# Gate tiles moved into five heads' turns, and one shared stationary key tile per score level for both chunks

## The chip, the core and the metric

The kernel runs on one core of a Trainium2 chip. Its engines work side by side and meet through semaphores: TensorE (PE) multiplies, VectorE (DVE), ScalarE (ACT) and GpSimd (POOL) work element by element, and SyncE (SP) issues DMA transfers. The metric is the device time of one execution in microseconds (us); lower is better. A kernel's time is the median of its runs.

## What is computed

One step of a decoder layer over 320 token columns: one prompt of 256 tokens and 8 samples of 8 tokens, width 2048, everything in float32. After a norm, one input projection with 5120 columns feeds a pooling mixer (1024 columns) and eight heads of a gated recurrence, 128 columns each for q, f, v (called i below) and the gate g. Both groups go through an output projection and a residual add, and then come a SwiGLU block with 5632 hidden columns and a last norm.

```python
u, q, f, i, g = split(rms_norm(x, norm1) @ w_in)
forget = lb + (1 - lb) * sigmoid(f)
k, v, q = 1 - forget, i, silu(q)
# per head and token: S_t = diag(forget_t) S_{t-1} + k_t^T v_t ;  o_t = q_t S_t
o, S_new = hgrn2_recurrence(q, k, v, log(forget), S_prev)
o = rms(o) * hg_norm * silu(g)
x = x + concat([pool_mix(u), o]) @ w_o
x = x + (silu(h2 @ w_gate) * (h2 @ w_up)) @ w_down        # h2 = rms_norm(x, norm2)
```

## The kernel before

**Dense tiles.** Activations lie in SBUF with features on partitions and the 320 tokens along the free axis. Every large product is cut into *units* (`unit`): one 128-column weight tile, 16 row blocks, and for each block three fp32r matmuls of 320 columns (high part of the weights with both parts of the activations, low part with the high part), so 48 matmuls. A unit's weight tile is loaded by SP into one of two buffers `w_raw`, ACT writes its high part `w_hi` in two pieces (`split_hi`), and DVE then writes the low part `w_lo` = `w_raw` - `w_hi` in two pieces (`split_lo`, `lo_piece`). Two PSUM banks take turns, and a unit may start only when the unit two before it has been read out; `unit_read` counts these reads.

**Order of the input projection.** Eight pooling units, then three units per head (f, q, v; the numbers H0 on), then eight gate units (G0 on), then sixteen units of the output projection (O0 on), then the SwiGLU block.

**A head.** In `window(n, parity, h, r)` each engine interleaves the three units of head h with the recurrence of the head before it, r. The recurrence is evaluated by levels: for each of 7 levels (block halves of 1, 2, ..., 64 tokens) the keys are scaled towards the end of their block and the queries from its start. The pieces, by the names in the traces:

- DVE reads the unit f out (`zf`), ACT makes the forget factors (`t`), DVE multiplies them up in `products` (seven small operations `t<-t`, semaphore `prod_ready`).
- POOL makes the keys in `keys`: `kx0` = 1 - forget, and for each level the next `kx` by one multiplication with `t`; then `query` (`qq<-zq,sgm`, the silu of q), then `key_copies` (written to `dg`), and, first in the next window, `rec_sample` (`sn<-s,t`, 1024 elements per partition, and `vm`). POOL works in this order.
- DVE scales the queries in `queries`: `qr0` and seven further levels, eight operations, the first of which waits for `qq`.
- PE multiplies in `rec_scores`: transposes of the last keys, then for every level and each of the two 128-token chunks of the prompt one matmul with the chunk's own `kx` level as stationary operand and the 64 queries of the right block halves moving; own-token and sample scores lie between; at the end transposes of v. It waits for `qr_ready` and `kx_ready`.
- DVE puts the scores into place with 12 predicated copies (`rec_scores` on DVE, `sc`, `scs`), and PE goes on with `rec_state`, `rec_out`, `rec_stat` (means of squares). DVE turns these into the norm (`rec_rms`, which ends with the diagonals `dg`), and `rec_bcast` on PE spreads them over the partitions: PE waits for `dg` there. `rec_norm` and `rec_lo` write the head's result.

`rec_scores` stands in the middle of the window's first unit on PE, `rec_state` behind it, `rec_out` in the middle of the second, `rec_stat` behind it, `rec_bcast` behind the third.

**A gate.** In `gate`, DVE reads the unit out, ACT takes its sigmoid, POOL multiplies (`zq<-zf,sgm`), DVE adds up the head's high and low part and multiplies (`gate_apply`), ACT writes the new high part and DVE the new low part. Nothing else runs beside most of the gate units.

What sets the order on each engine is the order of the code; nothing is scheduled.

Of the kernel before, what the change touches and what calls it, by code (L numbers as in the profile page):

```python
# [54 lines left out]
C_MP = C_ID + P  # L55
# [8 lines left out]
G0 = H0 + 3 * HEADS  # L64
O0 = G0 + HEADS
# [6 lines left out]
def constant_table(np):  # L72

    c = np.zeros((P, C_END), np.float32)
    c[:, C_ID:C_ID + P] = np.eye(P)
    s = np.arange(P)[:, None]
    for level in range(LP):
# [3 lines left out]
        for ch in range(NC):  # L81
            c[:, C_MP + level * P + ch * 64:C_MP + level * P + ch * 64 + 64] = m
# [10 lines left out]
def hybrid_kernel(nc, x_prompt, x_sample, cache_pool, state_hgrn, lb_param, norm1, w_in, w_pool, pool_scale,  # L93
# [12 lines left out]
    with ctx:  # L106
# [56 lines left out]
        kx = region(early, [(f"kx{l}", [P, N if l <= LS else TP], F32) for l in range(LP + 1)])  # L163
# [16 lines left out]
        go = vv  # L180
# [34 lines left out]
        zf_sig, f_ready, prod_ready, zq_sig, q_ready, qr_ready, kx_ready = (  # L215
            sem(n) for n in ("zf_sig", "f_ready", "prod_ready", "zq_sig", "q_ready",
                             "qr_ready", "kx_ready"))
# [26 lines left out]
        def thrice(rep, src):  # L244

            return (rep[:, 0:6 * HS].rearrange("p (i c t) -> p i c t", i=2, c=3),
                    src[:, TP:N].rearrange("p (i t) -> p i t", i=2).unsqueeze(2).to_broadcast([P, 2, 3, HS]))
# [13 lines left out]
        def times(level, n, lo):  # L261

            m = n // 2 ** (level + 1)
            return tl[level][:, 0:m, lo:lo + 2].unsqueeze(3).to_broadcast([P, m, 2, 2 ** level])

        def prod_in(level, which):

            m = (N if level < LS else TP) // 2 ** (level + 1)
            return tl[level][:, 0:m, which:which + 1].rearrange("p (m a) q -> p m (a q)", a=2)

# [21 lines left out]
        def _(sp):  # L292
# [21 lines left out]
            sp.dma_start(cst[:, C_MP:C_END], consts[:, C_MP:C_END]).then_inc(masks_loaded, 16)  # L314
# [5 lines left out]
            with sp.Fori(0, HEADS // 2) as i:  # L320
                for k in range(2):
                    for j, part in enumerate((2, 1, 3)):
                        load(H0 + 6 * i + 3 * k + j, (3 * k + j) % 2, win_v, (0, KD),
                             part * PW + (2 * i + k) * P)
            with sp.Fori(0, HEADS // 2) as i:
                for k in range(2):
                    load(G0 + 2 * i + k, k, win_v, (0, KD), 4 * PW + (2 * i + k) * P)
# [22 lines left out]
        def _(pe):  # L350
# [141 lines left out]
            def rec_scores(r):  # L492
# [3 lines left out]
                pe.transpose(TK[:, 0:P], kx[LP][:, 0:P], ident)  # L496
                pe.transpose(TK[:, P:TP], kx[LP][:, P:TP], ident)
# [7 lines left out]
                def level(bk, at, l):  # L505
                    for c in range(NC):
# [65 lines left out]
            def window(n, par_, r, extra=(None, None), last=False):  # L572

                def at(f):
                    return (lambda: f(r)) if r is not None else None
# [1015 lines left out]
```

## Time and profile before

| | us |
|---|---|
| median of 3 runs (1488.51 to 1493.13) | 1489.78 |
| the profiled execution's own time | 1493.66 |
| its span, first to last instruction | 1491.4 |
| PE / DVE / ACT / POOL busy in the span | 1460.7 / 804.9 / 550.8 / 188.2 |

The busy sums are of the whole span. The recurrence takes the stretch from about 122 us (scores of head 0) to 395 us (last spread of head 7); before and behind it PE runs dense units without a break. A matmul's record begins when it is issued and its end is modelled, so on PE the distance from start to start tells what one costs. One fp32 matmul leaves two records, one fp32r matmul one.

### The profile page before, as it was taken

The numbers are of one execution on the slowest core, as the hardware profiler recorded it, in microseconds if no ns is written. First come the engines' busy times: TensorE is split into PE (matmuls) and PEld (weight loads), VectorE is DVE, ScalarE is ACT, GpSimd is POOL, SyncE is SP. The second block draws the span as 40 slices with busy tenths as digits, with TensorE's granted clock in tenths as the row PEclk, the third lists the DMA queues.
The fourth block names the chain that finished last, engine by engine and source line by source line (L and its number), as shares of the span: only waits on it lengthen the run. The fifth ranks groups of instructions, "written<-read, shape, count | busy, mean of one in ns | idle before, by whom it ended". The sixth has DMA issues, their size and how long they took to land.

```text
span 1491.4 us, 27027 instructions
## 1 busy us (share of the span) xinstructions
PE 1460.7 (98%) x9928; PEld 1440.6 (97%) x9928; DVE 804.9 (54%) x1200; ACT 550.8 (37%) x823; POOL 188.2 (13%) x202
## 2 busy tenths in 40 slices
PE   7999999999999999999999999999999999999996
PEld 5999999999999999999999999999999999999996
DVE  4657788787665554444444444444444444444443
ACT  6443433344443343333333333333333333333443
POOL 0244434333112210000000000000000000000131
PEclk9999999999999999999999999999999999999998
DMA  8445444434455555554565555565554556555453
GB/s 222 136 127 143 128 127 131 114 114 138 114 162 143 153 144 153 141 160 125 146 187 142 141 142 141 144 164 153 157 141 134 151 146 164 154 151 141 119 148 114
DMA packets 409519, 214.52 MB, mean 144 GB/s; under 512 B 4093, under 2 KB 407757, under 8 KB 409420
## 3 DMA queue, kind: packets, MB, share of 16 engines
q1 hardware_dynamic: 391207, 203.52, 49.8%
q10 hardware_dynamic: 18277, 10.52, 2.5%
q8 instruction: 23, 0.38, 0.1%
q14 instruction: 12, 0.10, 0.0%
HBM read 206.14 MB, written 7.89 MB: 144 GB/s over the span
## 4 chain that ended last, share of the span: by engine, by line
PE 85%; DVE 9%; issue 3%; ACT 2%; DMA 1%; DVEq 0%; ACTq 0%; SPq 0%
PE bank L366 27%; PE bank L367 27%; PE bank L368 27%; DVE qr L1190 2%; DVE w_lo L1013 2%; DVE t L1177 1%; ACT w_hi L682 1%; DVE sc L1205 1%; PE bank L507 1%; DMA xt<-in_x_sample 1%; DVE sn L1249 0%; PE bank L462 0%; PE bank L410 0%; PE bank L538 0%; PE bank L412 0%
## 5 line engine op out<-in xcount | busy, mean ns | idle before, releaser
L366 PE MATMUL bank<-a_hi,w_hi 128*128 128x320 f32 x2048 | 642.4, 314 | 0.0
L367 PE MATMUL bank<-a_lo,w_hi 128*128 128x320 f32 x2048 | 636.1, 311 | 0.0
L368 PE MATMUL bank<-a_hi,w_lo 128*128 128x320 f32 x2048 | 635.9, 311 | 0.0
L1013 DVE TENSOR_TENSOR w_lo<-w_raw,w_hi 128x1024 fp32r<-128x1024 f32 (+1 forms) x416 | 467.3, 1164 | 150.3 <-ACT w_hi L682 149.5
L682 ACT ACTIVATE w_hi<-w_raw 128x1024 fp32r<-128x1024 f32 (+1 forms) x416 | 387.3, 967 | 158.6 <-PE bank L368 148.5
L366 PEld LDWEIGHTS bank<-a_hi,w_hi 128*128 128x128 f32 x2048 | 387.6, 189 | 2.4
L367 PEld LDWEIGHTS bank<-a_lo,w_hi 128*128 128x128 f32 x2048 | 387.7, 189 | 0.8
L368 PEld LDWEIGHTS bank<-a_hi,w_lo 128*128 128x128 f32 x2048 | 387.3, 189 | 0.0
L366 PE MATMUL bank<-h_hi,w_hi 128*128 128x320 f32 x704 | 217.7, 309 | 0.0
L367 PE MATMUL bank<-h_lo,w_hi 128*128 128x320 f32 x704 | 216.6, 308 | 0.0
L368 PE MATMUL bank<-h_hi,w_lo 128*128 128x320 f32 x704 | 216.5, 308 | 0.0
L367 PEld LDWEIGHTS bank<-h_lo,w_hi 128*128 128x128 f32 x704 | 132.0, 187 | 0.0
L366 PEld LDWEIGHTS bank<-h_hi,w_hi 128*128 128x128 f32 x704 | 132.0, 187 | 0.0
L368 PEld LDWEIGHTS bank<-h_hi,w_lo 128*128 128x128 f32 x704 | 131.9, 187 | 0.0
L1562 POOL TENSOR_TENSOR sq<-x 128x320 f32<-128x320 f32 x15 | 10.8, 720 | 903.1 <-DVE x L1399 903.1
L909 ACT ACTIVATE h_hi<-hid 128x320 f32 (+1 forms) x44 | 20.7, 472 | 238.3 <-DVE hid L1367 238.3
L1401 DVE TENSOR_TENSOR x_res<-x_res,bank 128x320 f32 (+1 forms) x48 | 23.4, 488 | 120.7 <-PE bank L368 120.7
L1022 DVE TENSOR_TENSOR zu<-bank,rms_bc 128x320 f32<-128x320 f32 x44 | 21.6, 491 | 120.3 <-PE bank L368 120.3
L905 ACT ACTIVATE sg<-zg 128x320 f32<-128x320 f32 x44 | 20.8, 472 | 175.5 <-DVE zg L1022 175.5
L1022 DVE TENSOR_TENSOR zg<-bank,rms_bc 128x320 f32<-128x320 f32 x44 | 21.6, 491 | 86.4 <-PE bank L368 86.3
L1498 POOL TENSOR_TENSOR kx<-kx,t 128x256 f32<-128x256 f32 (+1 forms) x56 | 48.7, 870 | 30.8 <-DVE t L1177 27.5
L366 PE MATMUL bank<-mp_hi,w_hi 128*128 128x320 f32 x128 | 39.4, 308 | 0.0
(218 smaller groups left out, 1186.5 us busy)
## 6 DMA issues: line engine op xcount, KB each, us to landing
w_raw<-in_w_gate SPq DMA_DIRECT2D x44, 1024.0 KB, 5.6
w_raw<-in_w_up SPq DMA_DIRECT2D x44, 1024.0 KB, 5.6
w_raw<-in_w_down SPq DMA_DIRECT2D x64, 704.0 KB, 4.8
w_raw<-in_w_in SPq DMA_DIRECT2D x39, 1024.0 KB, 5.8
w_raw<-in_w_o SPq DMA_DIRECT2D x16, 1024.0 KB, 6.1
s<-in_state_hgrn ACTq DMA_DIRECT2D x8, 512.0 KB, 4.3
out<-sn ACTq DMA_DIRECT2D x8, 512.0 KB, 7.2
xt<-in_x_prompt SPq DMA_DIRECT2D x3, 512.0 KB, 9.4
```

The lines of the kernel that those rows point to most:

```text
L366: pe.matmul(out, whi[:, par_, cols], r_hi, start=(k == 0), stop=False)
L367: pe.matmul(out, whi[:, par_, cols], r_lo, start=False, stop=False)
L368: last = pe.matmul(out, wlo[:, par_, cols], r_hi, start=False, stop=(k == last_k))
L507: last = pe.matmul(bk[:, at + c * 64:at + c * 64 + 64].rearrange("p (m j) -> p m j", j=2 ** l), kx[l][:, c * CH:(c + 1) * CH], right_half( ...
L682: act.activation(whi[:, par_, k0 * P:k1 * P], raw[:, par_, k0 * P:k1 * P], ACT.Copy)\
L905: act.activation(sg[:, :], zg[:, :], ACT.Silu).then_inc(gate_act, 1)
L909: act.activation(h_hi[:, j, :], hid[:, :], ACT.Copy).then_inc(hid_hi, 1)
L1013: dve.tensor_tensor(wlo[:, par_, cols], raw[:, par_, cols], whi[:, par_, cols].bitcast(F32), SUB)\
L1022: return dve.tensor_tensor(out, zb[par_][:, 0:N], rbc[:, :], MUL)
L1190: dve.tensor_tensor(blocks_of(qr[l + 1], l, n), blocks_of(qr[l], l, n), times(l, n, 0), MUL)\
L1401: dve.tensor_tensor(x1[:, j, :], x1[:, j, :], zb[par_][:, 0:N], ADD).then_inc(unit_read, 1)
L1498: pool.tensor_tensor(blocks_of(kx[l + 1], l, n), blocks_of(kx[l], l, n), times(l, n, 2), MUL)\
```

## The change

1. **Gate units move.** Five of the eight gate units stand in front of the f unit of the heads 2 to 6, so that these heads' windows have four units: g, f, q, v (`gate_window` on DVE and ACT, `EARLY = 5`). The gate of head i is computed in the window of head i + 2. Heads 0, 1 and 7 keep three units, and three gate units are left, beside the recurrence of head 7.
2. **One stationary tile per level.** For each level, `km` holds the left block halves of chunk 0 and, in the places of the right halves, those of chunk 1, whose tokens lie in reversed order. One matmul of 128 queries per level (64 of each chunk) takes the place of two with 64. The second half of v (`turned`), the masks and the own-token identity are reversed to match.
3. **Keys.** `kp` is scaled in place, level by level; POOL copies the two halves of `km` out of it before each level, chunk by chunk, and keeps the samples' keys apart (`ks`).

```diff
 PE:
-                    for c in range(NC):
-                        last = pe.matmul(bk[:, at + c * 64:at + c * 64 + 64]...,
-                                         kx[l][:, c * CH:(c + 1) * CH], right_half(qr[l][:, c * CH:(c + 1) * CH], l),
-                                         start=True, stop=True)
+                    return pe.matmul(bk[:, at:at + P].rearrange("p (m j) -> p m j", j=2 ** l),
+                                     km[l][:, :], right_half(qr[l][:, 0:TP], l), start=True, stop=True)
...
+            def window(n, par_, r, count):
+                unit(n, par_, a_rhs, between=(lambda: rec_scores(r, n), lambda: rec_state(r)))
+                unit(n + 1, 1 - par_, a_rhs, between=(lambda: rec_out(r), lambda: rec_stat(r)))
+                unit(n + 2, par_, a_rhs, between=(None, lambda: rec_bcast(r)))
+                if count == 4:
+                    unit(n + 3, 1 - par_, a_rhs)
...
+            window(H0 + 3, 1, 0, 3)
+            with pe.Fori(0, EARLY) as i:
+                window(W2 + 4 * i, 0, i + 1, 4)
+            window(W7, 0, HEADS - 2, 3)
+            def last_bcast(k):
+                if k == HEADS:
+                    rec_bcast(HEADS - 1)
+            unit(G0, 1, a_rhs, between=(lambda: rec_scores(HEADS - 1, G0), lambda: rec_state(HEADS - 1)))
+            unit(G0 + 1, 0, a_rhs, between=(lambda: rec_out(HEADS - 1), lambda: rec_stat(HEADS - 1)))
+            unit(G0 + 2, 1, a_rhs, after_tile=last_bcast)
 ACT:
+            def gate_window(n, g, h, r):
+                split_hi(n + 1, 1)
+                rec_tokens(r)
+                gate_sigmoid(g, n, r)
+                split_hi(n + 2, 0)
+                gate_split(g)
+                rec_squares(r)
+                load_s0(h)
+                rec_stores(r)
+                forget(h, n + 1, g + 1)
+                split_hi(n + 3, 1)
+                rec_std(r)
+                sigmoid_q(h, n + 2)
+                split_hi(n + 4, 0)
+                rec_hi(r)
 DVE:
+            def gate_window(n, g, h, r):
+                split_lo(n + 1, 1)
+                rec_scores(r)
+                rec_sample_lo(r)
+                gate_read(n, 0)
+                rec_state(r)
+                split_lo(n + 2, 0)
+                gate_apply(g)
+                rec_sample_state(r)
+                scaled(n + 1, 1, zf[:, :]).then_inc(unit_read, 1)
+                split_lo(n + 3, 1)
+                products(h)
+                rec_rms(r)
+                scaled(n + 2, 0, zq[:, :]).then_inc(unit_read, 1)
+                split_lo(n + 4, 0)
+                queries(h)
+                rec_norm(r)
+                rec_lo(r)
+                values(n + 3, 1)
...
+            split_lo(G0 + 1, 0)
+            rec_scores(HEADS - 1)
+            rec_sample_lo(HEADS - 1)
+            gate_read(G0, 1)
+            rec_state(HEADS - 1)
+            split_lo(G0 + 2, 1)
+            gate_apply(EARLY)
+            rec_sample_state(HEADS - 1)
+            gate_read(G0 + 1, 0)
+            split_lo(O0, 0)
+            gate_apply(EARLY + 1)
+            rec_rms(HEADS - 1)
+            gate_read(G0 + 2, 1)
 POOL, keys(h):
-                pool.tensor_tensor(kx[0][...], ones..., tl[0][:, :, 1:3], SUB).then_inc(kx_ready, 1)
+                spans = [(lambda ap: ap[:, 0:CH], 0, CH, 0), (second_turned, CH, CH, 1)]
+                for part, t0, n in [s[:3] for s in spans] + [(lambda ap: ap[:, TP:N], TP, NS)]:
+                    last = pool.tensor_tensor(part(kx0)..., ones..., tl[0][:, t0 // 2:(t0 + n) // 2, 1:3], SUB)
+                last.then_inc(kx_ready, 1)
                 for l in range(LP):
-                    n = N if l < LS else TP
                     pool.wait_ge(kx_ready, (LP + 1) * h + l + 1)
+                    for c in range(NC):
+                        last = pool.tensor_tensor(half_of(km[l][:, :], l, c), half_of(src[:, c * CH:(c + 1) * CH], l, c),
+                                                  one, MUL)
+                    last.then_inc(km_ready, 1)
                     if l:
                         pool.wait_ge(prod_ready, LP * h + l)
-                    pool.tensor_tensor(blocks_of(kx[l + 1], l, n), blocks_of(kx[l], l, n), times(l, n, 2), MUL)\
-                        .then_inc(kx_ready, 1)
+                        pool.wait_ge(km_ready, LP * h + l + 1)
+                    for part, t0, n, c in spans:
+                        if l:
+                            firsts = half_of(part(kp), l, 0)
+                            last = pool.tensor_tensor(firsts, firsts,
+                                                      tl[l][:, c * m:(c + 1) * m, 2:3].to_broadcast([P, m, 2 ** l]), MUL)
+                        else:
+                            last = pool.tensor_tensor(blocks_of(part(kp), 0, CH), ...)
+                    if l < LS:
+                        last = pool.tensor_tensor(blocks_of(ks[l + 1], l, NS), blocks_of(ks[l], l, NS),
+                                                  times(l, NS, 2, TP), MUL)
+                    last.then_inc(kx_ready, 1)
...
+            with pool.Fori(0, EARLY) as i:
+                rec_sample(i + 1)
+                gate(i)
+                keys(i + 2)
+                query(i + 2)
+                key_copies(i + 2)
```

The order of instructions on POOL, in the window of head 1: before, the keys are `kx<-ones_mat,t` and seven `kx<-kx,t`.

```order
L1481 TENSOR_TENSOR vm<-v,cst 96x512 x2
L1490 TENSOR_TENSOR kx<-ones_mat,t 128x320
L1498 TENSOR_TENSOR kx<-kx,t 128x320 x3
L1498 TENSOR_TENSOR kx<-kx,t 128x256 x4
L1504 TENSOR_TENSOR qq<-zq,sgm 128x320
L1511 TENSOR_TENSOR dg<-kx,ones_mat 128x192
```

And now the first half of the same keys (levels 0 to 3; `km` is the shared stationary tile, `kp` the running prompt keys, `ks` the samples'):

```order
L1546 TENSOR_TENSOR kx<-ones_mat,t 128x128 x2
L1546 TENSOR_TENSOR kx<-ones_mat,t 128x64
L1555 TENSOR_TENSOR km<-kx,ones_mat 128x64 x2
L1567 TENSOR_TENSOR kp<-kx,t 128x128 x2
L1570 TENSOR_TENSOR ks<-kx,t 128x64
L1555 TENSOR_TENSOR km<-kp,ones_mat 128x32x2 x2
L1564 TENSOR_TENSOR kp<-kp,t 128x32x2 x2
L1570 TENSOR_TENSOR ks<-ks,t 128x64
L1555 TENSOR_TENSOR km<-kp,ones_mat 128x16x4 x2
L1564 TENSOR_TENSOR kp<-kp,t 128x16x4 x2
L1570 TENSOR_TENSOR ks<-ks,t 128x64
L1555 TENSOR_TENSOR km<-kp,ones_mat 128x8x8 x2
```

The eight key operations of a head have become 34: 3 for `kx0`, 5 for each of the levels 0 to 2, 4 for each of the levels 3 to 6. `qq` still stands behind all of them.

DVE, in the loop of the heads, before: what stands between the last product `t` and the norm of the head before (`stat`), whose end PE's spread waits for.

```order
L1177 TENSOR_TENSOR t<-t 128x2
L1022 TENSOR_TENSOR zq<-bank,rms_bc 128x320
L1011 ISA
L1013 TENSOR_TENSOR w_lo<-w_raw,w_hi 128x1024
L1011 REGISTER_ALU
L1013 TENSOR_TENSOR w_lo<-w_raw,w_hi 128x1024
L1255 RECIPROCAL stat<-stat 128x3
L1082 TENSOR_TENSOR stat<-stat 128x3
```

Now, in the loop of the four-unit windows, the part ahead of the products (`on<-mh_hi,mh_lo` to `mh_lo` is the gate; `zf` is the f unit, now the second of the window):

```order
L1310 TENSOR_TENSOR on<-mh_hi,mh_lo 128x320
L1317 TENSOR_TENSOR on<-on,zq 128x320
L1059 TENSOR_TENSOR mh_lo<-on,mh_hi 128x320
L1283 TENSOR_TENSOR sn<-sn,bank 128x512 x2
L1048 TENSOR_TENSOR zf<-bank,rms_bc 128x320
L1037 ISA
L1039 TENSOR_TENSOR w_lo<-w_raw,w_hi 128x1024
L1037 REGISTER_ALU
L1039 TENSOR_TENSOR w_lo<-w_raw,w_hi 128x1024
L1204 REGISTER_ALU
L247 REGISTER_ALU
L1211 TENSOR_TENSOR t<-t 128x80x2
```

The f unit is read one unit later in the window; one weight split instead of two lies between it and the norm, and the split of the next unit's weights stands behind `zq`, ahead of the queries.

## Rows read from the trace of the kernel before

**Rows 1.** The page: busy shares, and the chain by engine.

```profile
PE 1460.7 (98%) x9928; PEld 1440.6 (97%) x9928; DVE 804.9 (54%) x1200; ACT 550.8 (37%) x823; POOL 188.2 (13%) x202
PE 85%; DVE 9%; issue 3%; ACT 2%; DMA 1%; DVEq 0%; ACTq 0%; SPq 0%
```

**Rows 2.** Who waited for whom, PE: waiting line, releaser: us, times, longest.

```profile
PE bank L397 <- DVE dg L1092: 4.4, 5, 1.0
PE bank L507 <- issue: 3.1, 6, 0.5
```

**Rows 3.** Timeline of PE: start us, us, line, operands, count.

```profile
300.61 0.39 PE L366 MATMUL bank<-a_hi,w_hi 128*128 128x320 f32 x1
...
315.17 0.71 PE L391 MATMUL bank<-mean_cols,dg 128*128 128x1 f32 x6
...
324.13 0.49 PE L397 MATMUL bank<-dg,ones_mat 128*128 128x128 f32 x2 [1.01 <-DVE dg L1092]
...
329.87 1.52 PE L507 MATMUL bank<-qr,kx 128*128 128x64 f32 x12 [0.52 <-issue]
...
332.40 2.00 PE L507 MATMUL bank<-qr,kx 128*128 128x64 f32 x16
334.23 0.28 PE L528 MATMUL bank<-cst,vv 128*128 128x128 f32 x1
...
334.60 0.39 PE L366 MATMUL bank<-a_hi,w_hi 128*128 128x320 f32 x1
```

**Rows 4.** Timeline of DVE over the same window.

```profile
306.61 0.42 DVE L1025 TENSOR_TENSOR k<-bank,k 32x256 fp32r<-32x256 f32 x1
307.06 0.49 DVE L1022 TENSOR_TENSOR zf<-bank,rms_bc 128x320 f32<-128x320 f32 x1
...
309.88 3.05 DVE L1013 TENSOR_TENSOR w_lo<-w_raw,w_hi 128x1024 fp32r<-128x1024 f32 x2 [1.75 <-ACT w_hi L682]
...
314.05 3.30 DVE L1177 TENSOR_TENSOR t<-t 128x160 f32<-128x160 f32 x7
...
322.50 0.16 DVE L1255 RECIPROCAL stat<-stat 128x3 f32<-128x3 f32 x1
...
323.99 0.48 DVE L1184 TENSOR_TENSOR qr<-qq,t 128x320 f32<-128x320 f32 x1
324.50 5.15 DVE L1190 TENSOR_TENSOR qr<-qr,t 128x320 f32<-128x320 f32 x7
...
332.36 2.36 DVE L1013 TENSOR_TENSOR w_lo<-w_raw,w_hi 128x1024 fp32r<-128x1024 f32 x2 [0.33 <-ACT w_hi L682]
```

**Rows 5.** Timeline of POOL over the same window.

```profile
309.14 0.72 POOL L1490 TENSOR_TENSOR kx<-ones_mat,t 128x320 f32<-128x320 f32 x1 [0.45 <-ACT t L777]
...
318.28 0.62 POOL L1498 TENSOR_TENSOR kx<-kx,t 128x256 f32<-128x256 f32 x1 [0.16 <-POOL kx L1498]
...
319.63 1.86 POOL L1504 TENSOR_TENSOR qq<-zq,sgm 128x320 f32<-128x320 f32 x1
325.35 0.54 POOL L1511 TENSOR_TENSOR dg<-kx,ones_mat 128x192 f32<-128x192 f32 x1 [3.85 <-PE bank L400]
325.85 2.15 POOL L1475 TENSOR_TENSOR sn<-s,t 128x1024 f32<-128x1024 f32 x1
```

**Rows 6.** Timeline of DVE, one product of two elements.

```profile
316.80 0.55 DVE L1177 TENSOR_TENSOR t<-t 128x2 f32<-128x2 f32 x1
```

**Rows 7.** Timeline of POOL, what runs beside it.

```profile
316.69 0.64 POOL L1498 TENSOR_TENSOR kx<-kx,t 128x256 f32<-128x256 f32 x1 [0.16 <-DVE t L1177]
```

**Rows 8.** Stretches: busy (count) of PE, PEld, DVE, ACT, POOL; clock, DMA, GB/s.

```profile
346.00:348.00 2.00, 2.00 (x9) 1.92 (x8) 2.00 (x4) 0.00 (x0) 0.00 (x0) 0.50 0.51 121
400.00:500.00 100.00, 100.00 (x684) 100.00 (x683) 58.85 (x69) 37.03 (x49) 19.23 (x25) 1.00 0.55 150
```

**Rows 9.** Timeline of POOL at the first head's keys.

```profile
106.39 0.72 POOL L1490 TENSOR_TENSOR kx<-ones_mat,t 128x320 f32<-128x320 f32 x1
```

**Rows 10.** Timeline of PE at the first head's scores.

```profile
124.50 1.55 PE L507 MATMUL bank<-qr,kx 128*128 128x64 f32 x12 [1.32 <-DVE mp_lo L1148]
```

More of the change, by code:

```diff
@@ L54 @@
 C_ID = 0
-C_MP = C_ID + P
+C_AI = C_ID + P
+C_MP = C_AI + P
 C_MS = C_MP + LP * P
@@ L63 @@
 H0 = PW // P
-G0 = H0 + 3 * HEADS
-O0 = G0 + HEADS
+EARLY = 5
+W2 = H0 + 6
+W7 = W2 + 4 * EARLY
+G0 = W7 + 3
+O0 = G0 + HEADS - EARLY
 F0 = O0 + KD
@@ L513, in rec_scores @@
                 last.then_inc(sc_mm, 1)
-                for c in range(NC):
-                    pe.matmul(SA[:, c * CH:(c + 1) * CH], kx[0][:, c * CH:(c + 1) * CH], qq[:, c * CH:(c + 1) * CH],
-                              start=True, stop=True)
-                last = pe.matmul(SA[0:NS, TP:N], kx[0][:, TP:N], qq[:, TP:N], start=True, stop=True)
+                for c, own in enumerate((kx0[:, 0:CH], kx0[:, CH:TP])):
+                    pe.matmul(SA[:, c * CH:(c + 1) * CH], own, qq[:, c * CH:(c + 1) * CH], start=True, stop=True)
+                last = pe.matmul(SA[0:NS, TP:N], ks[0], qq[:, TP:N], start=True, stop=True)
                 for l in range(LS):
                     last = pe.matmul(SA[0:NS, N + 32 * l:N + 32 * l + 32].rearrange("p (m j) -> p m j", j=2 ** l),
-                                     kx[l][:, TP:N], right_half(qr[l][:, TP:N], l), start=True, stop=True)
+                                     ks[l], right_half(qr[l][:, TP:N], l), start=True, stop=True)
                 last.then_inc(sc_mm, 1)
@@ L1269, in rec_lo @@
                 split_rest(bh_lo[:, r, :], on[:, :], bh_hi[:, r, :]).then_inc(mh_lo_s, 1)
-            def gate(n, par_, h):
-                gate_read(n, par_)
-                gate_apply(h)
             def gate_read(n, par_):
@@ L1340, in _ @@
-            rec_lo(HEADS - 1)
-            gate_apply(3)
-            with dve.Fori(0, (HEADS - 4) // 2) as i:
-                for k in range(2):
-                    split_lo(G0 + 5 + 2 * i + k, 1 - k)
-                    gate(G0 + 4 + 2 * i + k, k, 4 + 2 * i + k)
+                rec_sample_state(r)
+                products(h)
+                scaled(n + 1, 1 - par_, zq[:, :]).then_inc(unit_read, 1)
+                split_lo(n + 3, 1 - par_)
+                rec_rms(r)
+                queries(h)
@@ new lines, in _ @@
+            split_lo(H0 + 1, 1)
+            scaled(H0, 0, zf[:, :]).then_inc(unit_read, 1)
+            split_lo(H0 + 2, 0)
+            pool_means(NG - 1)
+            dve.wait_ge(t_ones, 1)
+            products(0)
+            scaled(H0 + 1, 1, zq[:, :]).then_inc(unit_read, 1)
+            split_lo(H0 + 3, 1)
+            queries(0)
+            pool_lo(NG - 1)
+            dve.wait_ge(sc_zero, 1)
+            values(H0 + 2, 0)
+            window(H0 + 3, 1, 1, 0)
+            with dve.Fori(0, EARLY) as i:
+                gate_window(W2 + 4 * i, i, i + 2, i + 1)
@@ L1496, in keys @@
                     if l:
                         pool.wait_ge(prod_ready, LP * h + l)
-                    pool.tensor_tensor(blocks_of(kx[l + 1], l, n), blocks_of(kx[l], l, n), times(l, n, 2), MUL)\
-                        .then_inc(kx_ready, 1)
+                        pool.wait_ge(km_ready, LP * h + l + 1)
[5 more added lines that the diff above has]
+                        else:
+                            last = pool.tensor_tensor(blocks_of(part(kp), 0, CH), blocks_of(part(kx0), 0, CH),
+                                                      times(0, CH, 2, t0), MUL)
```

232 lines of the change are left out of this document (104 added, 128 removed).

## Prediction

> **What bounds the kernel now.** I read the page first: PE is busy for 98% of the span, and the chain that ended last lies on PE for 85% and on DVE for 9% [rows 1]. Behind the recurrence PE issues 684 matmuls in 100 us [rows 8], so a unit of 48 costs 7.0 us and nothing waits. The question is the stretch of the heads. The waits of PE give two small ones per head there: for the diagonals `dg`, up to 1.0 us, and ahead of the score matmuls, up to 0.5 us [rows 2]. The timelines of one window show what the head is made of. From the first dense matmul behind one head's scores to the same place of the next it is 334.60 - 300.61 = 34.0 us [rows 3]. PE does three units (21.1) and about 11.3 of recurrence in it, and waits about 1.6. So PE bounds the heads too, but with little over: two chains on other engines arrive 0.5 and 1.0 us late already. I follow the one through POOL and the queries.
>
> Call Z the moment at which DVE begins to read the f unit, Q the end of the last `qr`, when PE may start the score matmuls. Before, Z = 307.06 and Q = 324.50 + 5.15 = 329.65, 22.6 us later [rows 4], and PE starts at 329.87 [rows 3]. In that chain POOL has room: `qq` ends at 321.49 [rows 5], and DVE, busy with the norm from 322.50 on, turns to `qr0` at 323.99 [rows 4]. From Q to the next Z (307.06 + 34.0 = 341.05) it is 11.4 us.
>
> **Part 1, half as many score matmuls.** 28 records of 64 columns become 14 of 128. The 16 records from 332.40 end where L528 starts, at 334.23: 0.114 us each [rows 3]. 128 columns aren't shown in this place; the lower bound is the same 0.11, the upper one the 0.147 of a 320-column matmul [rows 8]. I take the lower, the row nearest in kind (fp32, recurrence). That saves 14 x 0.114 = 1.6 us a head (1.1 at the upper bound), 12.8 over eight heads, all of it on PE. Whether it is worth anything depends on who is late at Q.
>
> **Part 2, the keys on POOL.** Eight operations of 320 or 256 elements become 34: two of 128 and one of 64 for `kx0`; two of 64, two of 128, one of 64 for level 0; five of 64 for levels 1 and 2; four of 64 for levels 3 to 6. The trace has 320 elements at 0.72, 256 at 0.62, 192 at 0.54 us [rows 5], so 64 elements fewer save 0.08 to 0.10 and most of a small operation is fixed cost. On that line 64 elements take 0.33 and 128 take 0.42; back to back they overlap by 0.04 (`dg` at 325.35 for 0.54, `sn` at 325.85 [rows 5]): 0.29 and 0.38. The bounds for 64 elements are 0.14 (in proportion to 0.72) and 0.54 (the smallest seen). Sum: 1.05 + 1.63 + 2 x 1.45 + 4 x 1.16 = 10.2 us. Each level waits once for POOL's own `kx_ready`, and from level 1 on once more for its own `km_ready`; such a wait costs 0.16 [rows 5]: 13 x 0.16 = 2.1. Together 12.3.
>
> The Trainium skill, page "GPSIMD Engine Reference", section 3.1, gives a two-input operation 2.6 cycles per element at 1.2 GHz, 2.17 ns. By that nearly all of 0.72 is slope and 64 elements would take some 0.17 us, 4 us less per head, and the kernel would come out near 1515. The trace has 1.6 ns between 256 and 320 elements, so I keep the fixed cost.
>
> POOL doesn't run alone. A DVE product of two elements lasts 0.55 us and ends at 317.35, just behind a POOL operation that ends at 317.33 [rows 6, 7]; the pair of `w_lo` takes 3.05 beside a key operation and 2.36 alone [rows 4]; `qq`, as large as `kx0`, takes 1.86 instead of 0.72 beside `w_lo` [rows 5]. So operations of DVE and POOL with both inputs in SBUF take turns, and each waits for the whole of the other. Between Z and `qq` DVE now has two weight splits (4.4), the products and the norm (small, some 1.2 of POOL's time together): 5.6. The keys start 2.1 behind Z (309.14 - 307.06 [rows 4, 5]) and end at Z + 20.0; `qq` is behind them in POOL's order, 0.9, so Z + 20.9. Only then come the queries: 5.7 us as before (323.99 to 329.65, with the 2.15 of `sn` in their way [rows 4, 5]), and 0.6 more, since `key_copies` now starts together with them. Q = Z + 27.2 instead of 22.6.
>
> **Windows of three units.** Q to Z stays 11.4. The cycle is 38.6 instead of 34.0: +4.6. There are two such steps (scores of head 0 to 1, of head 6 to 7): +9.2.
>
> **Windows of four units.** If PE set the pace, a cycle would be 34.0 + 7.0 - 1.6 - the waits of 1.6 = 37.8. Q to the reading of the gate is 11.4; from there to the reading of f it is 7.0 as from `zf` to the first `t` before [rows 4], less 1.5 (no `t` on ACT, no key operation in the way of `w_lo`), plus 2.0 for the gate itself (three operations of DVE and one of ACT at about 0.49): Z = Q + 18.9. PE would have the f unit done at Q + 18.0, so DVE is even. The cycle is 18.9 + 27.2 = 46.1, against 34.0 + 7.0 = 41.0 for a head and a gate unit before: +5.1, five times, +25.5. PE spends its surplus in two places. At the spread it arrives at Z + 7.4; DVE has waited for w_hi (to Z + 2.8 as before [rows 4]), then split, multiplied and normed, with POOL in every gap: Z + 11. That is a wait of 3.5 against 1.0. And ahead of the scores about 4 more. What is queued behind these two on PE is one unit and the rest of the window; the gate unit moved in covers the chain less well than it looks, because the f unit moved back with it: from f to the scores PE has two and a half units, as before.
>
> **First and last head.** The first keys start at 106.39, when POOL is done with the pooling windows [rows 9]. 12 + 5.6 + 0.9 gives `qq` at 124.7, eight queries at 0.5 and the two `mp_lo` behind them 129.4, against 124.50 [rows 10]: +4.9 - 1.6, about +3. At the end the norm of head 7 stands behind `gate_apply` of the second gate unit on DVE and ACT: about Q + 28.5, while PE comes to tile 8 of the last gate unit at Q + 22.6. Before, the spread had slack there. 6 less 1.6 and a little: +5.
>
> **Clock.** Just behind a head's small matmuls and a wait the granted clock is 0.50 of full, 1.2 GHz [rows 8]. Such 2 us lose 1 us. With waits of 4 us ahead of every scores, I add 4 us for the part that DVE's chain doesn't hide. The skill's page "TensorE: Matmul & The Clock Gate", section "HAM oscillation", says that waits that recur between bursts bring the clock down every time; by it up to 2 us a window, 10 in all, would be the term.
>
> **Sum.** 9.2 + 25.5 + 3 + 5 + 4 = +47 on the profiled execution's own 1493.7 (span 1491.4 and 2.3 around it), so 1541; that execution is 3.9 above the median, so the median becomes 1537. No other edit counts: the table of constants is 128 columns longer in an early transfer, v is read out in three pieces (+0.3 a head, inside Q to Z), SP's loads keep their order of two buffers.
>
> **Rivals.** (a) Faster: POOL's chain fits its cover. If 64 elements cost 0.17 and turns overlap in POOL's own waits, Q is at Z + 19, where PE arrives; then PE sets the pace, the kernel gains 12.8 and most of the waits of [rows 2] (7.5): 1470 to 1480. It decides at Q < Z + 19.4. For it: `qq` is ready 2.5 us early before. Against it: the turns seen in every window, and that even without any turn Q would be Z + 2.1 + 12.3 + 0.9 + 4 = 19.3. 8 in 100. (b) Only the spread is late: the queries fit, `dg` doesn't. Then each four-unit window costs about 2.5 us more wait at the spread and saves 1.6 and the 0.5 ahead of the scores: the sum of the five is near 0, and head 0, 7 and the ends make it 1488 to 1505. 10 in 100. (c) The forecast's mechanism, 1505 to 1560: 80 in 100. (d) Small POOL operations cost 0.4 and more, nearer the upper bound: 34 x 0.1 is 3.4 us a head, 1565 and above. 2 in 100.
>
> Range 1495 to 1560. From the same cases: no change means within 0.3% (about what a measurement here can tell), 1485 to 1494: 0.05; faster 0.08; slower 0.87.
>
> **What would show it.** Right: POOL's `km` and `kp` operations at about 0.3 us and its keys filling some 17 us of each window; `qq` ending 20 to 21 us behind `zf`; PE idle 3 to 6 us ahead of L523 (released by DVE `qr`) and 2 to 5 us ahead of the spread, released by `dg`; windows of 46 us; the clock at 0.50 in several windows. Wrong: L523 records at 0.15 or more, POOL operations of 64 elements at 0.2, or `qr` done before PE has its first half unit; then the windows would be near 38 us.

## The result, and the profile after

The kernel before takes 1491.45 us (median of 4 runs, 1488.51 to 1493.17), the changed kernel 1518.03 us (4 runs, 1515.53 to 1519.69): a ratio of 1.0179, with a 95% interval of 1.0155 to 1.0203. The forecast of 1537 (1495 to 1560) had the direction and the mechanism; the time came out 19 us below it. The profiled execution of the changed kernel took 1519.69 us, 26.0 more than the profiled one of before; its span is 1517.9 us, 26.5 more.

From the page of the changed kernel, the busy shares and the chain by engine, which answer to [rows 1]:

```profile
PE 1463.0 (96%) x9816; PEld 1441.3 (95%) x9816; DVE 792.6 (52%) x1214; ACT 560.7 (37%) x831; POOL 239.3 (16%) x410
PE 83%; DVE 6%; POOL 4%; issue 3%; ACT 2%; DMA 1%; ACTq 0%; DVEq 0%; POOLq 0%; SPq 0%
```

POOL issues 410 instructions instead of 202 and now stands in the chain. The waits of PE between 120 and 460 us (waiting line, releaser, us in total, times, longest) answer to [rows 2]:

```profile
PE bank L414 <- DVE dg L1126: 16.0, 6, 4.8
PE bank L523 <- issue: 11.6, 7, 2.7
PE bank L523 <- DVE mp_lo L1182: 4.0, 1, 4.0
```

The six waits at the spread (L414) are one of 4.8 us behind head 7 and five in the gate windows, which average 2.2 us; those ahead of the scores (L523) average 1.7 us. The page puts the latter down to "issue"; that they are waits for the queries follows from the times, since in every window from head 1 on the score matmuls start 0.2 us behind Q. In the timeline of PE one gate window goes from 300.29 to 343.95, against the 34.0 us of [rows 3]:

```profile
300.29 0.39 PE L383 MATMUL bank<-a_hi,w_hi 128*128 128x320 f32 x1
...
324.83 0.49 PE L414 MATMUL bank<-dg,ones_mat 128*128 128x128 f32 x2 [2.03 <-DVE dg L1126]
...
339.40 0.91 PE L523 MATMUL bank<-qr,km 128*128 128x128 f32 x6 [2.31 <-issue]
...
343.95 0.61 PE L383 MATMUL bank<-a_hi,w_hi 128*128 128x320 f32 x1
```

The timeline of DVE over it, which answers to [rows 4]: Z is 315.14 and Q is 334.23 + 4.97 = 339.20, 24.1 us later. PE starts the scores 0.2 us behind Q, after 2.31 us of idling.

```profile
315.14 0.48 DVE L1048 TENSOR_TENSOR zf<-bank,rms_bc 128x320 f32<-128x320 f32 x1
318.06 2.58 DVE L1039 TENSOR_TENSOR w_lo<-w_raw,w_hi 128x1024 fp32r<-128x1024 f32 x2 [2.44 <-ACT w_hi L695]
320.57 2.34 DVE L1211 TENSOR_TENSOR t<-t 128x160 f32<-128x160 f32 x7
322.83 0.16 DVE L1289 RECIPROCAL stat<-stat 128x3 f32<-128x3 f32 x1
...
324.50 0.28 DVE L1126 TENSOR_SCALAR dg<-cst,stat 64x64 f32<-64x64 f32 x1
...
333.41 0.78 DVE L1218 TENSOR_TENSOR qr<-qq,t 128x320 f32<-128x320 f32 x1 [4.16 <-POOL qq L1577]
334.23 4.97 DVE L1224 TENSOR_TENSOR qr<-qr,t 128x320 f32<-128x320 f32 x7
```

DVE stood idle for 4.16 us until POOL released it with `qq`. The timeline of POOL, which answers to [rows 5], shows what `qq` was queued behind:

```profile
317.31 1.02 POOL L1546 TENSOR_TENSOR kx<-ones_mat,t 128x128 f32<-128x128 f32 x3 [7.56 <-ACT t L791]
318.41 2.39 POOL L1555 TENSOR_TENSOR km<-kx,ones_mat 128x64 f32<-128x64 f32 x2
320.77 1.18 POOL L1567 TENSOR_TENSOR kp<-kx,t 128x128 f32<-128x128 f32 x2
...
330.13 0.54 POOL L1555 TENSOR_TENSOR km<-kp,ones_mat 128x64 f32<-128x64 f32 x2
330.75 0.55 POOL L1564 TENSOR_TENSOR kp<-kp,t 128x64 f32<-128x64 f32 x2
...
332.50 0.88 POOL L1577 TENSOR_TENSOR qq<-zq,sgm 128x320 f32<-128x320 f32 x1
333.34 0.51 POOL L1584 TENSOR_TENSOR dg<-ks,ones_mat 128x192 f32<-128x192 f32 x1
```

The keys last from 317.31 to 332.50, 15.2 us, where those of before were done 10.5 us behind their start (309.14 to 319.63 [rows 5]).

Where the 26.5 us of span lie, by the first dense matmul behind each head's scores in the timelines of PE (a gate window is set against a head's window and a gate unit of 7.04 us before):

| stretch | before | after | difference | forecast |
|---|---|---|---|---|
| up to head 0's | 131.53 | 133.56 | +2.0 | +3 |
| head 0's to head 1's | 33.71 | 34.60 | +0.9 | +4.6 |
| five gate windows | 169.36 + 35.2 | 219.71 | +15.1 | +25.5 |
| head 6's to head 7's | 33.83 | 36.46 | +2.6 | +4.6 |
| from there to the end | 1122.96 - 35.2 | 1093.57 | +5.8 | +5 |

### The profile page after: what moved, and what is told of

The parts are those of the page before. It is cut to its first block, busy times and chain, and to the rows that moved or that the text cites. A ratio compares the mean times of both kernels' runs of the same rounds, so it can differ in the third digit from the quotient of the medians.

```text
span 1517.9 us, 26905 instructions
## 1 busy us (share of the span) xinstructions
PE 1463.0 (96%) x9816; PEld 1441.3 (95%) x9816; DVE 792.6 (52%) x1214; ACT 560.7 (37%) x831; POOL 239.3 (16%) x410
## 4 chain that ended last, share of the span: by engine, by line
PE 83%; DVE 6%; POOL 4%; issue 3%; ACT 2%; DMA 1%; ACTq 0%; DVEq 0%; POOLq 0%; SPq 0%
PE bank L383 26%; PE bank L384 26%; PE bank L385 26%; POOL km L1555 2%; DVE qr L1224 1%; POOL kp L1564 1%; DVE w_lo L1039 1%; ACT w_hi L695 1%; PE bank L523 1%; DVE sc L1239 1%; DMA xt<-in_x_sample 1%; PE bank L551 0%; PE bank L479 0%; DVE sn L1283 0%; DVE t L1211 0%
## 5 line engine op out<-in xcount | busy, mean ns | idle before, releaser
L1039 DVE TENSOR_TENSOR w_lo<-w_raw,w_hi 128x1024 fp32r<-128x1024 f32 (+1 forms) x416 | 460.0, 1146 | 161.3 <-ACT w_hi L695 159.9
L1555 POOL TENSOR_TENSOR km<-kp,ones_mat 128x64 f32<-128x64 f32 x96 | 39.8, 435 | 3.8
L384 PE MATMUL bank<-mp_lo,w_hi 128*128 128x320 f32 x128 | 39.4, 308 | 0.0
```

The source lines that it names most:

```text
L384: pe.matmul(out, whi[:, par_, cols], r_lo, start=False, stop=False)
L1039: dve.tensor_tensor(wlo[:, par_, cols], raw[:, par_, cols], whi[:, par_, cols].bitcast(F32), SUB)\
L1555: last = pool.tensor_tensor(half_of(km[l][:, :], l, c), half_of(src[:, c * CH:(c + 1) * CH], l, c), one, MUL)
```

## The experiments

Twelve kernels, each timed beside the kernel before (medians of before 1490.4 to 1492.0). "Theory K" is the forecast's: POOL's longer chain of keys makes the queries late, and the second place of f in a gate window makes both chains later still.

**Gate windows alone.** Keys, `qq` and score matmuls as before; units, loads and the gate's steps as in the changed kernel.

```diff
-                for c in range(NC):
-                    last = pool.tensor_tensor(half_of(km[l][:, :], l, c), ..., one, MUL)
...
+                pool.tensor_tensor(blocks_of(kx[l + 1], l, n), blocks_of(kx[l], l, n), times(l, n, 2), MUL)
```

> The gate units stand in the heads' windows, keys and score matmuls are those of before. Theory K (the loss comes through POOL's key chain, which makes the queries late): POOL has eight key operations again, the queries end in time, only the wait at the spread (2.3 us) stays in five windows and the last head's (5 us): about +10 us on before, near 1502 us. Theory S (the loss is the spread's wait and the place of the gate; the shared key tiles themselves gain 12.8 us): near 1530 us, slower than the changed kernel.

Measured: 1523.5 us, ratio 1.022 (1.0183 to 1.0257). K, which asked for 1502, missed by 21 us; the time is near S's 1530. K was right that the queries come in time (one wait of 0.5 us for them is left), but the wait at the spread isn't 2.3 us: the six waits there sum to 25.4 us, against 4.4 before. The timeline of PE of this run, at one spread:

```profile
320.38 0.59 PE L411 MATMUL bank<-dg,ones_mat 128*128 128x128 f32 x2 [3.97 <-DVE dg L1124]
```

and that of DVE ahead of it:

```profile
308.67 0.49 DVE L1048 TENSOR_TENSOR zf<-bank,rms_bc 128x320 f32<-128x320 f32 x1 [2.23 <-PE bank L382]
311.51 3.05 DVE L1039 TENSOR_TENSOR w_lo<-w_raw,w_hi 128x1024 fp32r<-128x1024 f32 x2 [2.35 <-ACT w_hi L695]
314.48 3.29 DVE L1209 TENSOR_TENSOR t<-t 128x160 f32<-128x160 f32 x7
317.69 0.16 DVE L1287 RECIPROCAL stat<-stat 128x3 f32<-128x3 f32 x1
...
319.72 0.60 DVE L1124 TENSOR_SCALAR dg<-cst,stat 64x64 f32<-64x64 f32 x1
```

The factors are ready 320.32 - 308.67 = 11.7 us behind Z, against Z + 11 in the forecast's working. Split, products and norm take longer here than in the changed kernel (3.05, 3.29 and 2.6 instead of 2.58, 2.34 and 2.0 us): each small DVE step takes turns with a key operation of 0.6 to 0.7 us instead of 0.3. The move of the gate units is harmful by itself, by the spread, and the short POOL operations seem to soften that. The half clock has a part in it too: in this run DVE waits 2.23 us for PE at Z (row above), so PE sets the pace, and the mean granted clock is 0.985 against 0.992, an estimated 0.007 x 1512 = 11 us of PE's work. The traced execution was the fastest of the five, 1513.35 us. It is 6.6 us ahead of the traced kernel before already at head 0 (first dense matmul behind the scores at 124.89 against 131.53), ahead of any gate window; why isn't known.

**Shared key tiles alone**, gate units behind the heads (the edit is against the changed kernel).

```diff
-W2 = H0 + 6
-W7 = W2 + 4 * EARLY
-G0 = W7 + 3
+G0 = H0 + 3 * HEADS
```

> The shared key tiles and the 34 POOL operations alone; all eight gate units stand behind the heads as before. Theory K: each step from head to head is 1 to 2.6 us longer (34.6 and 36.5 us for the three-unit windows of the changed kernel against 33.8), and 2 for the first: +9 to +20 us, near 1505 us. Theory S: PE saves 12.8 us and nothing else moves: near 1479 us.

Measured: 1504.1 us, ratio 1.0092 (1.0064 to 1.012): K. The waits of PE over 120 to 460 us:

```profile
PE bank L517 <- issue: 20.2, 7, 3.4
PE bank L517 <- DVE mp_lo L1163: 4.0, 1, 4.0
```

2.9 us ahead of the scores of each of the heads 1 to 7, with half as many matmuls behind it. The parts alone cost 12 and 32 us and together 26, so they don't add up. A likely reading is that each lengthens a chain that the other already makes PE wait for, and that the short operations relieve DVE; no run takes the two apart.

**Query early.** The changed kernel, POOL's `qq` ahead of level 4 of its keys.

```diff
                 pool.wait_ge(kx_ready, (LP + 1) * h + l + 1)
+                if l == 4:
+                    query(h)
                 for c in range(NC):
...
             keys(h)
-            query(h)
             key_copies(h)
```

> The changed kernel, with POOL's qq ahead of level 4 of the keys instead of behind level 6, nothing else. Theory K: qq is ready some 5 us earlier, DVE begins the queries behind its weight split, the wait ahead of the scores (about 2.4 us in seven windows) goes: 1518 - 17 = 1501 us. Theory S: the spread's wait is untouched: 1518 us.

Measured: 1493.45 us, ratio 1.0019 (1.0 to 1.0039): 24.6 less than the changed kernel, for moving one operation. K asked for 1501; the gain is 8 us larger, and no run here takes these 8 us apart. Its waits of PE:

```profile
PE bank L414 <- DVE dg L1126: 15.8, 6, 5.5
PE bank L513 <- POOL dg L1586: 2.4, 1, 2.4
```

The waits for the queries are gone, those for the factors stand as before.

**Factors first.** The changed kernel, `rec_rms` ahead of the products on DVE in the gate windows.

```diff
                 split_lo(n + 3, 1)
-                products(h)
                 rec_rms(r)
+                products(h)
```

> The changed kernel, with the norm (rec_rms) ahead of the products on DVE in the four-unit windows. The diagonals are ready about 2.3 us earlier, so PE's wait at the spread (2 to 3 us, five times) goes. Theory S: -11 us, near 1507 us. Theory K: PE then waits as much longer ahead of the scores, since the keys' and queries' chain from the reading of f sets the pace, and the products, and with them level 1 of the keys, start 1.7 us later: 1518 to 1523 us.

Measured: 1524.8 us, ratio 1.0229 (1.0192 to 1.0265): 6.8 more than the changed kernel. S is out; K's direction holds, its range is missed by 2. Its waits of PE:

```profile
PE bank L523 <- issue: 27.8, 7, 4.5
PE bank L414 <- DVE dg L1126: 5.6, 2, 4.8
```

The wait for the factors shrinks from 16.0 to 5.6 us, and that for the queries grows from 11.6 to 27.8: what stands in series is DVE's and POOL's chain, and a wait of PE taken away in one place comes back at the next.

**Filled waits.** The changed kernel with extra matmuls where PE waits.

```diff
+            def fill(bk):
+                for i in range(14):
+                    pe.matmul(bk[:, 0:N], a_hi[:, i, 0:P], a_hi[:, i, :], start=True, stop=True)
...
+                fill(SA)
                 pe.wait_ge(q_ready, r + 1)
...
+                fill(TK)
                 pe.wait_ge(odiag, r + 1)
```

> The changed kernel (1518.0 us) with 14 extra matmuls of 320 columns (0.146 us each, 2.05 us) on TensorE ahead of its wait for the queries and 14 ahead of its wait for the norm's factors, in every head; their results are read by nobody. In the changed kernel both waits last 2.4 to 3 us, so the extra matmuls end before the waits do. Theory C (the clock): the changed kernel has ten stretches of 3.4 us at half clock that the kernel before has not, worth about 10 x 1.7 = 17 us, and they come because TensorE idles in these waits; with the waits filled they go: about 1501 us. Theory K (the chain of keys and queries sets the time, TensorE at full clock would only wait the longer): within 3 us of 1518, and where a wait is shorter than 2.05 us, up to 4 us more.

Measured: 1518.4 us, ratio 1.0181 (1.0145 to 1.0218): K. The cores' view (span, mean granted clock) of before, of the changed kernel and of this one:

```profile
core 0: 1491.4 us, clock 0.992
```

```profile
core 0: 1517.9 us, clock 0.981
```

```profile
core 0: 1516.9 us, clock 0.990
```

The clock is nearly back, the time is not. On paper the changed kernel's lower clock is worth (0.992 - 0.981) x 1518 = 17 us of PE's work, two thirds of the loss, and (0.990 - 0.981) x 1517 = 14 of them are restored here. So most of the low clock is a consequence of the waits and costs nothing where PE would wait anyway.

It isn't quite free, and this run doesn't put it at zero. Where a wait is shorter than the fill, the fill itself delays PE: head 1's scores start at 167.69 us against 163.41 in the changed kernel. By head 7's the difference is down to 0.3 us (419.88 and 419.58). Part of what was made up is in the last gate window: in the changed kernel it takes 45.2 us from scores to scores (heads 5 to 6) where the three before it take 43.9, and in this run it is 43.9 as well. In that window PE runs at 1.2 GHz (0.50) twice, and DVE waits for its f unit. DVE's timeline of the changed kernel:

```profile
360.50 0.49 DVE L1048 TENSOR_TENSOR zf<-bank,rms_bc 128x320 f32<-128x320 f32 x1 [1.42 <-PE bank L385]
```

**One copy.** The changed kernel without the second chunk's copy into the shared tiles in heads 1 to 7, so that its scores for that chunk come from stale keys.

```diff
-                    for c in range(NC):
+                    for c in range(chunks):
...
-                keys(i + 2)
+                keys(i + 2, 1)
```

> The changed kernel with the second chunk's copy into the shared key tiles left out for heads 1 to 7 (7 POOL operations of 64 elements a head; the score levels of the second chunk are then computed from stale keys). It shortens POOL's chain ahead of the query by 7 x 0.27 to 0.33 us = 1.9 to 2.3 us a head. Theory K (in every one of the seven windows the time hangs on that chain, directly where TensorE waits for the queries, and elsewhere where its half clock stands in for the wait): 7 x 2.1 = 15 us less, about 1503 us (1500 to 1507). Rival F (what the change costs is the wait for the norm's factors, which these copies do not lengthen): within 3 us of 1518.

Measured: 1506.5 us, ratio 1.0107 (1.0089 to 1.0125). 11.5 us less, of the 15 that K asked for and against none by F. Its waits of PE show why it isn't all:

```profile
PE bank L414 <- DVE dg L1126: 17.4, 6, 5.5
PE bank L523 <- DVE mp_lo L1182: 4.0, 1, 4.0
PE bank L523 <- issue: 1.5, 2, 1.0
```

With some 2 us less on POOL the queries come nearly in time, and the factors become the bound.

**No table load at the loop's start.** In the changed kernel ScalarE loads a function table once more per pass. Its timeline there:

```profile
339.78 0.47 ACT L844 ACTIVATE mh_hi<-on 128x320 f32 x1 [12.20 <-DVE on L1298]
340.28 1.28 ACT L695 ACT_TABLE_LOAD   x1
341.58 2.00 ACT L695 ACTIVATE w_hi<-w_raw 128x1024 fp32r<-128x1024 f32 x2
```

```diff
             window(H0 + 3, 1, 1, 0)
+            act.activation(warm[:, 1:2], epst[:, 0:1], ACT.Sigmoid)
             with act.Fori(0, EARLY) as i:
```

> The changed kernel with one Sigmoid of a single column on ScalarE ahead of the loop over the gate windows, so that ScalarE holds the same table at the loop's entry and at its end, and the two loads of 1.28 us (before the first w_hi of a pass, and before the gate's sigmoid) go. Theory K+T (the first of these loads stands in the cycle from one head's queries to the next head's f unit, which paces the gate windows): 1.28 us less in each of 5 passes, about 1518 - 6 = 1512 us. Rival (the load lies beside other work, only TensorE's waits count): within 2 us of 1518.

Measured: 1516.6 us (1514.0 to 1518.1), ratio 1.0169 (1.0134 to 1.0204). That is inside the rival's 2 us of 1518. In the profiled execution the span is 3.7 us shorter (1514.2), and all of that in the five gate windows; the medians differ by 1.4 only, inside the spread of four runs each. So the load's place in the cycle is seen, and its worth is small: between 0 and 4 us, not the 6 of K+T. DVE's timeline of this run has a query's end at 289.27 + 4.96 = 294.23 and the next Z at 312.99, 18.8 us:

```profile
289.27 4.96 DVE L1225 TENSOR_TENSOR qr<-qr,t 128x320 f32<-128x320 f32 x7
...
312.99 0.48 DVE L1049 TENSOR_TENSOR zf<-bank,rms_bc 128x320 f32<-128x320 f32 x1
```

Two of the four steps from Q to Z between gate windows are 18.8 us long in this run. The other two are still 19.8: there DVE waits 0.96 and 0.93 us at Z for PE, which has run part of the window at 1.2 GHz (0.50).

**Gate windows alone, factors first.** The first experiment with the order of the fourth.

> The gate windows alone, with keys and score matmuls of before (gate windows alone measured 1523.5 us), with the norm's factors ahead of the products on DVE. Theory K (two causes: in the gate windows alone the factors come some 4 us late behind the products, and the queries late behind the second f unit; the order takes the first away, and moves products, keys and queries back by 1.5 us): 1500 to 1510 us, still over the kernel before. Rival G (the products' order is the whole of the gate windows' cost): 1488 to 1494 us, the same as the kernel before. Rival H (the queries become as late as the factors were): 1518 to 1525 us.

Measured: 1513.3 us, ratio 1.0157 (1.0136 to 1.0178), 10 less than the gate windows alone. G and H are out; K's range is missed by 3. Its waits of PE:

```profile
PE bank L521 <- issue: 11.2, 7, 2.1
PE bank L411 <- DVE dg L1124: 5.2, 2, 4.8
```

Even with the keys of before the gate units inside the heads make both chains late, one or the other by the order. The waits are 9 us more than before, though, and the span is 18 us more. The rest is about what the half clock costs: the mean granted clock is 0.986 against 0.992, an estimated 0.006 x 1510 = 9 us of PE's work. The windows show it. From scores to scores the heads 2 to 4 take 41.5 us, the heads 4 to 6 45.9, with PE at 1.2 GHz (0.50) behind the scores, and there DVE waits for PE at Z:

```profile
307.32 0.49 DVE L1048 TENSOR_TENSOR zf<-bank,rms_bc 128x320 f32<-128x320 f32 x1 [3.77 <-PE bank L382]
```

**Both orders** on the changed kernel: query early and factors first.

> The changed kernel with POOL's query ahead of level 4 of its keys and the norm's factors ahead of the products, without the changed table load and without the changed end (with all four: 1480.4 us). Theory K (the two orders carry nearly all of it; the changed end is worth some 3 us and the table load 1 to 2): 1483 to 1487 us. Rival T (with the waits gone the table load of 1.28 us stands in the cycle of every pass): 1488 to 1491 us.

Measured: 1485.4 us (9 runs), ratio 0.9966 (0.9953 to 0.9978): K. The two orders together, one of which alone made the changed kernel slower (1524.8), bring it 0.3% below the kernel before.

**All four orders:** also without the table load, and with the last head's factors ahead of the gate product that stood before them at the end.

```diff
-            gate_apply(EARLY + 1)
             rec_rms(HEADS - 1)
+            gate_apply(EARLY + 1)
+            dve.wait_ge(gm_lo, EARLY + 2)
```

> The changed kernel with four orders changed: POOL's query product ahead of level 4 of the keys (alone 1493.5 us), the norm's factors ahead of the products on DVE in the gate windows, no table load at the loop's start, and at the end the last head's factors ahead of the last gate product but one. Theory K (in the query-early kernel 5 waits of about 2.5 us for the factors are left, and at the end 5 us; the factors first takes them away without delaying the queries past TensorE, since these now end 3 us sooner): 1493.5 - 5 x 2.3 - 3 = about 1479 us (1474 to 1485). Rival (the factors first puts the products and with them POOL's keys back by the 1.4 us that the queries can't spare, as it did in the kernel with the factors first alone): 1488 to 1495 us.

Measured: 1480.4 us, ratio 0.9938 (0.9904 to 0.9971): K. What PE still waits for in it:

```profile
PE bank L513 <- POOL dg L1588: 6.9, 5, 2.3
PE bank L414 <- DVE dg L1127: 2.7, 2, 1.9
```

L513 is the transposes of the last keys, which wait for POOL to finish these and their copies (`dg`): with the queries in time, PE still waits 1.4 us a gate window for the end of POOL's chain.

**Shared key tiles and query early, no gate move.**

> The shared key tiles alone (gate tiles behind the heads, as before), with POOL's product of the query ahead of level 4 of its keys. Keys alone measured 1504.1 us. Theory K (what keys cost is that DVE's queries come late behind POOL's longer chain; without that only TensorE's saving of 1.6 to 1.8 us a head is left): 1479 to 1484 us, faster than the kernel before (1492). Rival S2 (TensorE's stage is bound elsewhere in a three-unit window, by w_lo or the norm, as soon as the queries are in time): 1489 to 1495 us.

Measured: 1468.0 us (1467.7 to 1469.4), ratio 0.9847 (0.9814 to 0.9879): the fastest, 22 us under the kernel before measured beside it (1490.4), and 11 better than K's range, which had counted the matmuls alone. One window of it, timeline of PE:

```profile
283.20 0.39 PE L377 MATMUL bank<-a_hi,w_hi 128*128 128x320 f32 x1
...
305.75 0.49 PE L408 MATMUL bank<-dg,ones_mat 128*128 128x128 f32 x2
...
310.82 0.83 PE L517 MATMUL bank<-qr,km 128*128 128x128 f32 x6
...
313.97 0.39 PE L377 MATMUL bank<-a_hi,w_hi 128*128 128x320 f32 x1
```

30.8 us instead of 34.0. From the first score matmul to the dense ones it is 313.97 - 310.82 = 3.15, against 334.60 - 329.87 = 4.73 [rows 3]: 1.6 us of matmuls, at full clock in both. The other 1.6 are the two waits of [rows 3], 0.52 and 1.01, both gone. The second goes with DVE's shorter steps ahead of the factors: its products take 2.21 us in this run instead of 3.30 [rows 4], and the weight split behind them 2.47 instead of 3.34:

```profile
296.62 2.21 DVE L1192 TENSOR_TENSOR t<-t 128x160 f32<-128x160 f32 x7
```

**The kernel before with the query early**, to see whether the order alone is worth it.

```diff
+                    if l == 5:
+                        query(h)
                     if l:
                         pool.wait_ge(prod_ready, LP * h + l)
```

> The kernel before with its query product on POOL ahead of the keys' last two levels, its seven key tiles and its score matmuls as they were. The shared key tiles with the query early measured 1468.0 us, 23 us less than the kernel before (1491). Theory K (the 23 us are the shared tiles' own: about 1.8 us of matmuls and 0.5 us of wait ahead of the scores a head, and 1.0 us ahead of the norm's factors, since POOL's short operations hold DVE's products up less, 2.21 instead of 3.30 us for the seven; in the kernel before the query is late by at most the 0.5 us wait): 1487 to 1492 us. Rival O (the order is what pays, whatever the tiles): 1475 to 1483 us.

Measured: 1492.2 us (10 runs), ratio 1.0003 (0.9981 to 1.0025): no change, K within 0.2, and O is out. The 22 us belong to the shared tiles; the order only lets them through.

## Why the forecast was right, and where its sizes were off

**Matmul saving, 1.6 us a head.** Right: 1.6 by the rows above. In the changed kernel it is spent on waiting and on half clock: in the window shown at the top the scores take 343.95 - 339.40 = 4.55 us instead of 3.15, with the granted clock at 0.50 from 341 on.

**POOL's chain.** Forecast: keys of 12.3 us alone and 17.9 with the turns, `qq` at Z + 20.9. Measured: 15.2 and Z + 18.2 (333.38 - 315.14). This is the term that was mis-sized most. Of the 21 us by which the sum of +47 exceeds the 26 measured, the windows have 16 (10 in the gate windows, 6 in those of three units), the clock's term up to 4. The operations themselves were right: two of 64 elements take 0.54 to 0.58 us, 0.27 to 0.29 each, as taken. Too much were the waits on POOL's own semaphores (0.08 us: the pair at 330.13 ends at 330.67 and the next starts at 330.75; I had taken the 0.16 of [rows 5] thirteen times: 1.0 too much), the two weight splits (`km` in 2.39 instead of 0.55 us is 1.8 for a split, not 2.2: 0.7 too much) and the products and the norm (the remaining 1.0). The Trainium skill, page "GPSIMD Engine Reference", section 3.1, gives 2.6 cycles per element for a two-input operation; the estimate from it in the forecast, 0.17 us for 64 elements, would have made the chain 4 us shorter yet. The measured 0.27 to 0.29 shows that this slope alone doesn't hold for short operations.

**Q.** Forecast Z + 27.2, measured Z + 24.1: the 2.7 above, and 5.8 us from `qq`'s end to Q instead of 6.3.

**Q to the next Z in a gate window.** Forecast 18.9, measured 19.8 in three of the four steps between gate windows and 21.3 in the last (339.20 to 360.50). What I had not seen is ScalarE's load of 1.28 us at the loop's start; without it the run above has 18.8 in two of them. The cycle is 43.9 (219.71 / 5) instead of 46.1.

**The two waits.** Forecast 3.5 at the spread and about 4 ahead of the scores; measured in the gate windows 2.2 and, ahead of the scores, 0.4 to 2.3, below the 3 to 6 that "what would show it" asked for. The kind is right; the size is smaller by the shorter chain, and because part of PE's surplus went into half clock instead of waiting. That the chain of DVE and POOL and not PE sets the pace in the changed kernel's gate windows, but for the last of them, is shown by the scores starting 0.2 us behind Q in each and by three runs: one wait removed comes back at the other (factors first), most of the clock restored leaves the time (filled waits), a shorter chain shortens the windows (one copy).

**Windows of three units.** Forecast +4.6 each, measured +0.9 and +2.6. By the same correction of 3.1 it would be +1.5 each; the mean is 1.75.

**First and last head.** +2.0 and +5.8, forecast +3 and +5. (The forecast's sum for the first head's `qq` gives 124.9, not 124.7; measured is 122.99.) The last wait, in the timeline of PE of the changed kernel:

```profile
448.53 0.79 PE L414 MATMUL bank<-dg,ones_mat 128*128 128x128 f32 x2 [4.78 <-DVE dg L1126]
```

**Clock.** +4 us were added. What the trace of the changed kernel shows of it is the 1.4 us that DVE waits at 360.50; the filled waits leave room for a few us more, since their fills delay the first heads. The stretch of [rows 8], read as "behind small matmuls and a wait", follows the small matmuls alone: the last wait ahead of it ended at 329.87. The Trainium skill, page "TensorE: Matmul & The Clock Gate", section "HAM oscillation", has waits between bursts bring the clock down every time. The trace agrees in that the mean is 0.981 instead of 0.992, and 0.990 with the waits filled. What a low clock costs depends on who paces the loop: little in the changed kernel, some 9 us in the gate windows alone with the factors first, where DVE waits for PE.

**Rivals.** (a), POOL's chain fits, decided at Q < Z + 19.4: not met here. Query early meets it in the gate windows (Q at Z + 18.5 to 18.9) and still takes 1493.5, not 1470 to 1480, since the factors stay late: the condition alone wasn't enough. With all four orders it is 1480.4, and without the gate move 1468.0, below (a)'s 1470. I had treated the place of `qq` in POOL's order as given, while only `qq`, not the keys, was late for DVE. (b), only the spread late: query early measures it almost purely, 1493.5 in its 1488 to 1505. (d) is out: operations of 64 elements take 0.29 to 0.35 us, and those above were beside one of DVE.

## What to carry to other kernels

When a change splits a helper engine's work into more, smaller operations, look at what is queued behind them on that engine: here one operation of 0.9 us behind 34 short ones turned a gain of 22 us into a loss of 12. Before adding up a loop's waits, find which engine's chain closes the cycle; a wait or a low clock on an engine that isn't in it costs little or nothing, and taking one away only moves it. Then look again in each variant: with another order the same engine can be the one that sets the pace. And two changes that are bad alone by a shared chain can't be judged by their sum: measure each with the order that suits it.

## What the runs showed of the hardware

- Short operations of POOL hold DVE up less than long ones. The seven products of DVE take 3.29 to 3.30 us beside key operations of 0.6 to 1.0 us and 2.21 to 2.34 beside those that are mostly 0.3, which fits turns of whole operations.
- A wait of POOL on its own semaphore cost 0.08 us in the changed kernel and 0.16 before.
- In this kernel the loop whose entry and end leave ScalarE with different function tables has a load of 1.28 us at the start of every pass, ahead of a plain copy; with the same table on both sides (no table load) the copy runs without it.
- 14 us' worth of TensorE's clock restored left the changed kernel's time where it was (1518.4 against 1518.0, four runs each within 5 us), fills included. Where PE paces the loop the clock counts: windows of 45.9 us at half clock behind the scores against 41.5 without, in the gate windows alone with the factors first.
